# Two expert layers in one run of ten tiles, with the second mixer's work placed between their steps

## The reference

```python
for layer in range(2):
    a = modulate(rmsnorm(h, mix_norm_g[layer]), sh1, sc1)     # latent and context tokens
    h = h + g1 * mixer(a)              # layer 0: retention + short convolution; layer 1: attention
    f = modulate(rmsnorm(h, ffn_norm_g[layer]), sh2, sc2)
    h = h + g2 * peer_ffn(f)
return rmsnorm(h_lat, final_norm_g)
```

```python
act = gelu(einsum('td,thkd->thk', x, u_tab[expert]))
y = einsum('thk,thkd->td', softmax(score) * act, v_tab[expert])
```

## Time and profile before

| | |
|---|---|
| three executions, us | 4126.82, 4129.3, 4130.6 (median 4129.3) |
| the profiled execution, us | 4134.11 |
| its span, first to last instruction, us | 4132.1 |
| mean granted TensorE clock | 0.955 of full |
| busy, share of the span | PE 81%, DVE 64%, POOL 39%, ACT 37%, weight loads 37% |
| moved | 1455.21 MB, 352 GB/s over the span |

### The profile page before, as it was taken

How to read it: one execution, slowest core, us unless ns; L and a number is a source line. 1 busy time by engine, 2 the same in 40 slices (tenths; PEclk the granted TensorE clock), 3 DMA queues, 4 the chain that set the end, 5 groups by cost and what they waited for, 6 DMA issues and landing times. The chain is left out here.

```text
span 4132.1 us, 32412 instructions
## 1 busy us (share of the span) xinstructions
PE 3351.1 (81%) x9736; PEld 1531.3 (37%) x9736; DVE 2632.1 (64%) x6027; ACT 1508.4 (37%) x4394; POOL 1603.7 (39%) x1482
## 2 busy tenths in 40 slices
PE   4998878788788778779777877887888877977776
PEld 0894633233233233223322226663333322322222
DVE  3314398866866875875874544658886686587444
ACT  3220143343343343344333332534334334333333
POOL 0005044444444444444444331323444444444332
PEclk7999999999999999999999998998999999999999
DMA  8117289999999999999999983027999999999997
GB/s 359 51 62 276 107 357 396 421 422 421 418 421 419 413 412 420 418 412 420 413 413 422 421 365 105 11 82 315 394 421 421 421 418 421 419 409 417 422 421 330
DMA packets 215391, 1455.21 MB, mean 352 GB/s; under 512 B 25920, under 2 KB 25920, under 8 KB 44080
## 3 DMA queue, kind: packets, MB, share of 16 engines
q0 software_dynamic: 184704, 1342.31, 78.5%
q1 hardware_dynamic: 30400, 110.72, 7.2%
q10 hardware_dynamic: 112, 0.11, 0.0%
HBM read 1447.72 MB, written 5.34 MB: 352 GB/s over the span
## 5 line engine op out<-in xcount | busy, mean ns | idle before, releaser
L1463 PE MATMUL peer_py<-peer_ring,peer_diag 128*128 128x512 f32 x5120 | 2514.8, 627 | 616.9 <-ACT peer_diag L1393 605.7
L1346 POOL DMA_INDIRECT peer_ring<-in_uv_dram,peer_idx x1280 | 1455.0, 1137 | 1819.0 <-PE peer_py L1463 1703.2
L1563 DVE CUSTOM_DVE_ANT_0 peer_ring<-peer_ring,peer_f 128x1024 f32<-128x1024 f32 x1280 | 1556.1, 1225 | 924.6 <-DMA peer_ring<-in_uv_dram,peer_idx 916.1
L1463 PEld LDWEIGHTS peer_py<-peer_ring,peer_diag 128*128 128x128 f32 x5120 | 930.4, 195 | 2153.5 <-ACT peer_diag L1393 1318.8
L1387 ACT ACTIVATE peer_gel<-peer_u 128x1 f32<-128x1 f32 x1280 | 258.9, 202 | 1832.2 <-DVE peer_u L1563 1830.8
L1393 ACT ACTIVATE peer_diag<-ident,peer_coef 128x128 f32<-128x128 f32 x1280 | 513.9, 402 | 41.7
L1391 ACT ACTIVATE peer_coef<-peer_gel,peer_gate 128x1 f32<-128x1 f32 x1280 | 377.2, 295 | 46.4
L353 DVE TENSOR_TENSOR m_w_low<-m_w_low_plain,m_w_high 128x2048 fp32r<-128x2048 f32 x26 | 61.0, 2348 | 218.4 <-ACT m_w_high L348 218.4
L361 PE MATMUL m_ps<-m_w_high,m_aT_high 128*128 128x512 f32 x416 | 165.7, 398 | 3.5 <-DVE m_v L820 1.8
L1438 PE MATMUL peer_pb<-arena,peer_fT 128*128 128x512 f32 x320 | 163.1, 607 | 2.4 <-ACT peer_fT L1360 2.4
L361 PE MATMUL m_ps<-m_w_low,m_aT_high 128*128 128x512 f32 x416 | 163.5, 393 | 0.0
(11 more groups left out here) (194 smaller groups left out, 2364.4 us busy)
## 6 DMA issues: line engine op xcount, KB each, us to landing
mod_rows_sb<-in_ada_w_dram SPq DMA_DIRECT2D x33, 1024.0 KB, 5.0
peer_ring<-in_uv_dram,peer_idx POOLq DMA_INDIRECT x1280
arena<-in_ada_w_dram SPq DMA_DIRECT2D x15, 1024.0 KB, 16.0
m_w_low_plain<-in_ev_w_in_dram SPq DMA_DIRECT2D x12, 1024.0 KB, 5.1
arena<-in_peer_wq_dram SPq DMA_DIRECT2D x2, 4096.0 KB, 19.2
mod_rows_sb<-mod_rows SPq DMA_DIRECT2D x7, 1024.0 KB, 6.9
m_w_low_plain<-in_od_w_in_dram SPq DMA_DIRECT2D x6, 1024.0 KB, 5.2
m_w_low_plain<-in_ev_w_out_dram SPq DMA_DIRECT2D x4, 1024.0 KB, 5.0
```

What stands on the lines that cost most here:

```text
L1346: pool.indirect_dma_start(ring[:, n % RING], None, A["uv"], bass.IndirectOffsetOnAxis(idx[:, i % 2, hd, k:k + 1], 0)).then_inc(sem(f"lande ...
L1463: ins = pe.matmul(PY[:, i % 2, b], diag[:, n % RING], ring[:, n % RING, D + b * HALF:D + (b + 1) * HALF], start=s == 0, stop=s == TS - 1)
L1563: dve.tensor_tensor_reduce(x, x, f[:, i % 2], 1.0, 0.0, ALU.mult, ALU.add, u[:, n % RING:n % RING + 1]).then_inc(sem("dot"), 1)
```

## The change

`expert_stage` takes the place of `peer_stage`, `mixer1_stage` and `peer_stage`. It is one run of `LOOPS` = 10 loops of 128 steps: loops 0 to 5 are layer 0's tiles, loops 6 to 9 layer 1's. The ring, the gathers, the dots, the weights and the combines are as before. Between the steps of loops 1 to 6 the mixer's work for the tile that was just finished is done: norm, transpose, the product for keys and values, rotary angles, keys transposed (`key_tile`). Between the steps of loops 4 to 7 it is a block of 128 queries (`query_block`): query product at steps 36 to 51, from step 51 one of eight head pairs every five steps (`pair_step`), the output product at steps 97 to 112. A part of a pair stands a given number of steps after its start: logits 2, exponentials 3, reciprocal and shares 4, transposes (`spread`) 6, their copies 7, values 8, output 9.

Products are plain fp32, without split. Weights come in 176 pieces of 128x512 (256 KB, two transfers of 64 rows each) through a ring of three, `W_RING`, issued by SP. For PSUM the mixer uses the half of `PY` that the tile at hand does not use (`spare`) and `PB`. To make room, probabilities have one buffer (`pr`) that shares its memory with `fT`, `q` and `qT`; the transposed ones (`pT`) share theirs with `y` and `qtok`; the diagonals have 4 slots instead of 8; keys and queries of layer 1 are kept in the context tiles of `h`. The chain semaphores of DVE are joined into one (`linked`, `wait_links`), in the other stages as well; their instructions stay.

The diff, cut to its core:

```diff
-def mixer1_stage(nc, S, A, h, ident, mod_d, arena, rows):
...
+LOOPS = NT + LT
+W_RING = 3
+SQUARE, MEAN, ROOT, SCALED, TURN_K, MODULATE_K = 5, 7, 8, 10, 12, 14
+KV_FROM, KV_READ, K_TURN, K_KEPT = 17, 26, 28, 30
+Q_SCALED, TURN_Q, MODULATE_Q = 27, 31, 33
+Q_FROM, Q_ROPE, Q_TURN, Q_KEPT = (36, 44), (45, 53), (47, 55), (49, 57)
+PAIRS, PAIR_FROM, PAIR_STEP = ATT_HEADS // 2, 51, 5
+LOGITS, PROBS, INVERSE, SHARES, SPREAD, SPREAD_READ, VALUES, OUTPUT = 2, 3, 4, 4, 6, 7, 8, 9
+O_FROM, O_READ = (97, 105), (106, 114)
+BAND = P + 2 * 128
+KEYS, WIDE = CTX + BAND, CTX + BAND + 1
...
+def key_tile(i):
...
+    return i - 1 if 1 <= i <= NT else None
...
+def query_block(i):
...
+    return i - CT - 2 if CT + 2 <= i < CT + 2 + LT else None
...
+def pair_step(s, part):
+    p, left = divmod(s - PAIR_FROM - part, PAIR_STEP)
+    return p if left == 0 and 0 <= p < PAIRS else None
...
+def weight_pieces(i):
+    out = []
+    if key_tile(i) is not None:
+        out += [("od_w_in", k, 2 * HALF) for k in range(KC)]
+    if query_block(i) is not None:
+        out += [("od_w_in", k, c * HALF) for c in range(2) for k in range(KC)]
+        out += [("od_w_out", m, c * HALF) for c in range(2) for m in range(PAIRS)]
+    return out
...
+def expert_stage(nc, S, A, h, ident, mod_d, arena, rows):
...
+        shared = sb("shared", [P, 2 * D])
+        fT = shared[:, 0:D].rearrange("p (k n) -> p k n", k=KC)
+        q = shared[:, D:D + HALF]
+        qT = shared[:, D + HALF:2 * D].rearrange("p (k n) -> p k n", k=NH // 2)
+        pr = shared[:, 0:2 * WIDE].rearrange("p (x n) -> p x n", x=2)
+        mask = shared[:, 2 * WIDE:2 * WIDE + KEYS]
...
+        turn = sb("turn", [P, D + HALF])
+        y, qtok = turn[:, 0:D], turn[:, D:D + HALF]
+        pT = turn[:, 0:2 * KEYS].rearrange("p (x n) -> p x n", x=2)
+        diag = sb("diag", [P, RING // 2, P])
...
+        w = sb("w", [P, W_RING, HALF])
...
+        def spare(i):
+            return PY[:, (i + 1) % 2]
...
+            def piece(n, name, k, at):
+                if n >= W_RING:
+                    sp.wait_ge(msem("w_used"), n - W_RING + 1)
+                buf = w[:, n % W_RING]
+                for x in range(2):
+                    half = slice(x * HD, (x + 1) * HD)
+                    if name == "od_w_in":
+                        row = k * P + x * HD
+                    else:
+                        row = pair_heads(k)[x] * HD
+                    sp.dma_start(buf[half], A[name][0, row:row + HD, at:at + HALF]).then_inc(msem(f"w{n % W_RING}"), 16)
...
+                todo = weight_pieces(i)
+                for m, (name, k, at) in enumerate(todo):
+                    if i == CT + 2 and m == 3 * KC:
+                        sp.wait_ge(sem("s_ps"), 2 * NT)
+                        load_ahead_for_peer(sp, S, A, mod_d, arena, 1)
+                    piece(pieces_to(i) + m, name, k, at)
...
+            def sinks(b, m):
+                if m:
+                    pool.wait_ge(msem("probs"), 2 * (b * PAIRS + m))
+                else:
+                    pool.wait_ge(sem("s_ps"), 2 * (b + CT + 2) + 4)
+                for x, hd in enumerate(pair_heads(m)):
...
+            def shares(b, m):
+                pool.wait_ge(msem("recip"), b * PAIRS + m + 1)
+                for x in range(2):
+                    pool.tensor_scalar(pr[:, x, 0:n_keys(b)], pr[:, x, 0:n_keys(b)], st[:, 2, x:x + 1], 1.0, ALU.mult, ALU.mult
+                                       ).then_inc(msem("shares"), 1)
...
+            pool.wait_ge(msem("consts"), 80)
...
+                    m = pair_step(at, -1)
+                    if m is not None:
+                        sinks(b, m)
+                    m = pair_step(at, SHARES)
+                    if m is not None:
+                        shares(b, m)
...
+                act.wait_ge(sem("coef"), 2 * n + 2)
+                if n >= RING // 2:
+                    act.wait_ge(sem("slot_free"), n - RING // 2 + 1)
+                act.activation(diag[:, n % (RING // 2)], ident[:], ACT.Copy, scale=coef[:, at]).then_inc(sem("diag"), 1)
...
+                m = pair_step(s, OUTPUT)
+                if m is not None:
+                    act.wait_ge(msem("o"), b * PAIRS + m + 1)
+                    act.activation(xT[:, m], OUT, ACT.Copy).then_inc(msem("oT"), 1)
+                m = pair_step(s, PROBS)
+                if m is not None:
+                    act.wait_ge(msem("sink"), 2 * (b * PAIRS + m) + 2)
+                    for x in range(2):
+                        act.wait_ge(msem("logits"), 2 * (b * PAIRS + m) + x + 1)
+                        act.activation(pr[:, x, 0:n_keys(b) + 1], pr[:, x, 0:n_keys(b) + 1], ACT.Exp, bias=st[:, 0, x:x + 1], scale=-1.0,
+                                       accum_out=st[:, 1, x:x + 1]).then_inc(msem("probs"), 1)
+                m = pair_step(s, SPREAD_READ)
+                if m is not None:
+                    act.wait_ge(msem("pT_ps"), 2 * (b * PAIRS + m) + 2)
+                    ins = act.activation(pT[:, 0, 0:HALF], spare(i)[:, 0], ACT.Copy)
+                    if n_keys(b) > HALF:
+                        ins = act.activation(pT[:, :, HALF:KEYS], TAIL.rearrange("p (x n) -> p x n", x=2), ACT.Copy)
...
+                    if key_tile(i - 1) is not None:
+                        pe.wait_ge(msem("kT"), key_tile(i - 1) + 1)
+                    if query_block(i - 1) is not None:
+                        pe.wait_ge(msem("pT_even"), PAIRS * (query_block(i - 1) + 1))
+                        pe.wait_ge(msem("pT_odd"), PAIRS * (query_block(i - 1) + 1))
...
+            def product(i, m, out, x):
+                n = pieces_to(i) + m
+                pe.wait_ge(msem(f"w{n % W_RING}"), 32 * (n // W_RING + 1))
+                pe.matmul(out, x, w[:, n % W_RING], start=m % KC == 0, stop=m % KC == KC - 1).then_inc(msem("w_used"), 1)
...
+            def attend(b, m, i):
+                hd = b * PAIRS + m
+                if m:
+                    pe.wait_ge(msem("logits"), 2 * hd)
+                else:
+                    pe.wait_ge(sem("s"), 2 * (i + 2))
+                    pe.wait_ge(msem("kT"), min(i, NT))
...
+            def spread(b, m, i):
+                hd = b * PAIRS + m
+                if hd:
+                    pe.wait_ge(msem("pT_even"), hd)
+                    pe.wait_ge(msem("pT_odd"), hd)
+                    pe.wait_ge(msem("oT"), hd)
+                if m == 0:
+                    pe.wait_ge(msem("qT"), 2 * b + 2)
+                for x in range(2):
+                    pe.wait_ge(msem("shares"), 2 * hd + x + 1)
+                    for t in range(len(key_tiles(b))):
+                        out = spare(i)[:, x, t * P:(t + 1) * P] if t < 4 else TAIL[:, x * P:(x + 1) * P]
+                        ins = pe.transpose(out, pr[:, x, t * P:(t + 1) * P], ident[:])
+                    ins.then_inc(msem("pT_ps"), 1)
...
+            def values(b, m):
+                hd, tiles = b * PAIRS + m, key_tiles(b)
+                pe.wait_ge(msem("pT_even"), hd + 1)
+                pe.wait_ge(msem("pT_odd"), hd + 1)
...
+                m = pair_step(s, LOGITS)
+                if m is not None:
+                    dve.wait_ge(msem("sinks"), 1)
+                    dve.wait_ge(msem("mask"), 3 * (b + 1))
+                    dve.wait_ge(msem("S"), b * PAIRS + m + 1)
+                    if b * PAIRS + m:
+                        dve.wait_ge(msem("pT_ps"), 2 * (b * PAIRS + m))
+                    for x, hd in enumerate(pair_heads(m)):
+                        n = n_keys(b)
+                        both = PB[:, 0:3].rearrange("p b n -> p (b n)")[:, x * KEYS:x * KEYS + n]
+                        dve.tensor_tensor_reduce(pr[:, x, 0:n], both, mask[:, 0:n], -SCALE, sink[:, 1, hd:hd + 1], ALU.add, ALU.min,
...
+                m = pair_step(s, INVERSE)
+                if m is not None:
+                    dve.wait_ge(msem("probs"), 2 * (b * PAIRS + m) + 2)
+                    if b * PAIRS + m:
+                        dve.wait_ge(msem("shares"), 2 * (b * PAIRS + m))
+                    dve.reciprocal(st[:, 2], st[:, 1]).then_inc(msem("recip"), 1)
+                m = pair_step(s, SPREAD_READ)
+                if m is not None:
+                    dve.wait_ge(msem("pT_ps"), 2 * (b * PAIRS + m) + 2)
+                    if b * PAIRS + m:
+                        dve.wait_ge(msem("o"), b * PAIRS + m)
+                    dve.tensor_copy(pT[:, 1, 0:HALF], spare(i)[:, 1]).then_inc(msem("pT_odd"), 1)
...
+                    mixer(i, s)
...
-        peer_stage(nc, S, A, h, ident, mod_d, arena, rows, 0, 0, 0, NT)
-        mixer1_stage(nc, S, A, h, ident, mod_d, arena, rows)
-        peer_stage(nc, S, A, h, ident, mod_d, arena, rows, 1, CT, NT, LT)
+        expert_stage(nc, S, A, h, ident, mod_d, arena, rows)
```

821 lines of the change are left out of this document (371 added, 450 removed).

## The result

The change runs at **4220.9 us** (4215.6 to 4229.3) against 4129.95 in the same series of runs: ratio 1.022 (95% interval 1.020 to 1.024). The prediction, 4011 and faster, was wrong by 210 us and on the wrong side. The profiled execution has a span of 4217.5 us (before 4132.1), granted clock 0.954.

The account below looks back on a forecast made before the run. The prediction took the DMA gathers to set the pace, with a hole at the second mixer. 4134.1 - 350.6 + 132 + 100 = 4015.5, or 4011 us at the runs' median; 8-in-10 range 3920 to 4125.

Parts of the forecast that it names:

- Term 1: Seam between the expert layers: one run of ten tiles closes the second mixer's hole in the gathers, minus 350.6 us.
- Term 2: Bytes added to the full DMA queue: 176 weight pieces 120 us, other moved loads 12 us, together plus 132 us.
- Rival (e): At the seam: the run stops because tile 6 needs the finished block 0, about 4110 us; chance 0.03.
- Term 3: Engines inside the run: eight head pairs a block lag the gathers, 25 us a block, four blocks, plus 100 us.
- The chain as a mechanism: Head pairs: ACT, PE and DVE wait on each other in a closed loop, 17.6 us a pair against 12.6.
- The ring's credit: Gathers landing ahead during the head pairs give back about 6 slots of 2.5 us, 15 us a block.
- The preparation of the query rows: Steps 25 to 36 of block tiles, rows turned and modulated beside the key part: forecast to cost nothing.
- (a): Head pairs: the ring covers them and DMA remains the bound throughout, 3911 us; chance 0.13.
- (b): Head pairs: PE's clock falls, 1.5 us a pair at granted 0.9, about 4060; 4125 at 0.77; chance 0.16.
- (c): Head pairs: 64 ACT table switches cost 2.66 us, 1.38 more each, 4100 us; chance 0.04.
- (d): Weight pieces come late behind gathers already given, up to 4630 us; decides from 0.67 us a piece; chance 0.12.
- What would show it: Signs in the profile: no hole, tiles 0 to 3 at 322 to 328 us, block tiles 365 to 375, pairs 17 to 18.

## Why the prediction was wrong

- **What bounds the kernel, Term 1 (-350.6):** right. The hole went, plain tiles behind the blocks stayed at 322 us (tile 0 took 330.9 for 323.6, which Term 2's 12 us for moved loads can hold), and POOL's new wait for the column loads was hidden (first gather at 529.1, before 529.6). Rival (e) did not come.
- **Term 2 (+120 for pieces):** the step that failed most: 242. "I take 120, nearer the second, since it too is loads in rows of 2 KB and up" priced a piece by the length of its rows. What set the price was where its two DMAs write: 64 rows each in one half of the partitions, 1.4 us in stretches of their own, 0.73 as one DMA of 128 rows. With whole rows the kernel came to 4065.9 and the pieces to 94 us. The price of the q1 row could not have shown it: of its 110.7 MB not one was moved while gathers ran.
- **Term 3 (+100):** 186 without piece traffic. The chain as a mechanism was right, and its 17.6 us near: with the clock held a pair takes 18.1 in the middle blocks and 17.1 in the edge ones. That the mean comes so close is in part luck, as 17.6 was added up from rows of 640 keys, the middle blocks' form: there PE's part, from the diagonal to DVE's next logits, took 8.3 us for 7.7. The term was mis-sized elsewhere. The ring's credit, 15 us a block, was 4.5 (42 us missing in four blocks). Two things of it show in the run without traffic: the gathers landed ahead of DVE's dots rose from 1 at step 40 to 5 or 6 in the pairs and were back at 2 by step 100, so the lead was of four or five and not six; and in steps 97 to 112 PE needs 2.57 us a step, where an output product stands beside each combination, more than the gathers' 2.5. What each took of the credit is not isolated. The preparation of the query rows, "nothing", was 29. The pairs' stretches exceeded 160 by 15, of which the fallen clock took some 12.
- **The sum:** 186 - 100 = 86 and 242 - 120 = 122 make 208, for the 204 by which the span missed the sum (4217.5 against 4132.1 - 350.6 + 132 + 100 = 4013.5).
- **Rivals.** (a) fell: DMA share 0.83 in the pairs. (b) came true in its sign, granted 0.91, but it counted 1.5 us for each of 32 pairs, 48 us, and holding the clock gave back 12.5: a slow combination before the exponentials is hidden beside them, one behind them costs 1.7, in ten of 32 pairs of the kernel with whole rows. (c) fell: the load takes 1.28 us and the exponential follows after 0.02; the drain that the Trainium skill ("ScalarE: Activation LUTs", What ACT_TABLE_LOAD costs) adds to each switch, no row shows. (d) had the right side and mostly the wrong place: late landings were 42 us, and 200 came from slow gathers and pieces. The excess of 0.67 us a piece by which it was to decide is what happened: 242/176 = 1.37 for 0.68. The Trainium skill ("DMA: Bandwidth & Descriptors", Queues, rings and completion order) has engines go round their queues packet by packet. The counts fit that, 193 packets of gathers and 179 of pieces in 2414 to 2420 us, but in which turns an engine took them no row shows, and the rule says nothing of what a packet then costs.
- **What would show it:** "tiles with a block at 365 to 375" was the sign: 404 to 429, and tiles 1 to 3, where only eight pieces stand, 336 for 322 to 328. These alone would have given 1.5 to 1.7 us a piece.

Open: how much of the chain could be saved. PE lies close under it: it is busy 121.6 of the 158 us of a block's pairs, 14.4 us a pair of 18.7, slow combinations included, and so takes over when ACT's part is made shorter, as the run without table switch shows. No run has a held clock and no table loads. Why the last pair of a block is long in the tight order, and where the credit of the ring went in full, is open too.

## What to carry to other kernels

A transfer added to full DMA engines has a second price, on the transfers beside it, and where its rows land sets that. Let every DMA write rows across all partitions (here 128 rows at once, 0.73 us for 1.43), from one run of rows in memory, even if the host must lay weights out for it. A load's price is read from rows in which it ran beside the same neighbours, or measured in a kernel of transfers alone. Where an engine's work in a step is as long as the bottleneck's (here 2.57 us for 2.5), a lag is not recovered in that step, and a ring gives little credit. A chain that waits for one engine has a second engine close under it; before a link is shortened, look how long the next one would wait.

## Unexpected of the hardware

- The same 64 rows of 2 KB cost 0.82, 0.42 or 0.89 us beside gathers, written to partitions from 0, 32 or 64 on.
- Two DMAs of 64 rows of 2 KB raise a gather's 8 KB packet from 317 to 389 ns; one of 128 rows leaves it at 320.
- One DMA into 128 partitions whose source is two groups of 64 rows had two packets in flight at a time, and PE waited up to 16.0 us for it.
- PE's granted clock fell to half behind waits of 2 to 3 us in one head pair, and 1.5 and 0.9 us of unread transposes in those waits held it at 0.99.
